# Sliding-window attention of a three-layer kernel: keys and values first, queries in quarters, output units and scalings at other steps

## The reference

```python
def swa_mixer(h, w_qkv, sinks, w_o):            # h: 256 x 1024, rms-normed
    qkv = h @ w_qkv                             # 1024 x (1024 + 128 + 128)
    q, k, v = split(qkv)                        # 16 heads of 64, 2 of 64, 2 of 64
    s = einsum(q, k_with_previous_block) * 64 ** -0.5
    logits = where(mask, s - slope * dist, -1e30)
    m = maximum(max(logits), sink)
    p = exp(logits - m)
    probs = p / (sum(p) + exp(sink - m))
    return einsum(probs, v_with_previous_block) @ w_o
h = h + swa_mixer(rms_norm(h), ...)
h = h + relu(rms_norm(h) @ w_up) ** 2 @ w_down
```

## Time and profile before

| | us |
|---|---|
| median of 3 runs | 976.29 (975.81 to 977.70) |
| the profiled execution | 973.68 |
| its span, first to last instruction | 971.9 |
| TensorE busy in the span | 944.2 |
| GpSimd busy | 675.4 |
| ScalarE busy | 499.6 |
| VectorE busy | 451.1 |

### The profile page before, as it was taken

The page is one execution under the profiler, slowest core; times in us unless marked ns, Lnnn a source line. Parts: engine busy times, 40 slices in busy tenths (PEclk is TensorE's granted clock), DMA queues, the critical chain, the costliest instruction groups (busy, mean ns, idle before and its releaser), DMA issues.

```text
span 971.9 us, 17687 instructions
## 1 busy us (share of the span) xinstructions
PE 944.2 (97%) x6878; PEld 880.7 (91%) x6878; DVE 451.1 (46%) x867; ACT 499.6 (51%) x702; POOL 675.4 (69%) x486
## 2 busy tenths in 40 slices
PE   5989999999999999999999999999998999999997
PEld 5989999999998889999999999888896789998886
DVE  3448753378443242666565566616627352221003
ACT  4675342673225465555666556555557346554331
POOL 4886645467555797966766676667697549889883
PEclk9999999999999999999999999999999999999999
DMA  8989858969734565744434444455663237666641
GB/s 242 164 214 103 185 104 85 161 109 100 145 107 128 184 195 158 211 131 134 149 114 146 138 146 132 131 171 186 173 204 102 70 107 225 207 176 209 198 133 43
DMA packets 131243, 146.30 MB, mean 151 GB/s; under 512 B 11022, under 2 KB 95960, under 8 KB 131160
## 3 DMA queue, kind: packets, MB, share of 16 engines
q1 hardware_dynamic: 129176, 140.64, 57.6%
q10 hardware_dynamic: 1984, 4.53, 1.4%
HBM read 144.10 MB, written 1.05 MB: 149 GB/s over the span
## 4 chain that ended last, share of the span: by engine, by line
PE 85%; DVE 4%; POOL 3%; ACT 3%; DMA 2%; issue 2%; SPq 1%; DVEq 0%; ACTq 0%; POOLq 0%
PE dense L546 23%; PE dense L547 22%; PE dense L548 22%; PE bank L908 3%; DMA raw<-in_w_in_even_dram 2%; PE bank L804 2%; PE bank L807 2%; POOL wlo L521 1%; POOL wlo L520 1%; PE bank L822 1%; POOL lg L506 1%; DVE cv L1739 1%; PE bank L897 1%; ACT whi L1153 1%; PE dense L615 1%
## 5 line engine op out<-in xcount | busy, mean ns | idle before, releaser
L521 POOL TENSOR_TENSOR wlo<-raw,whi 128x512 fp32r<-128x512 f32 (+1 forms) x263 | 411.7, 1571 | 29.0 <-ACT whi L1153 29.0
L520 POOL TENSOR_TENSOR wlo<-raw,whi 128x512 fp32r<-128x512 f32 x199 | 259.3, 1303 | 233.1 <-ACT whi L1153 220.9
L1153 ACT ACTIVATE whi<-raw 128x1024 fp32r<-128x1024 f32 x264 | 276.4, 1058 | 269.9 <-PE dense L548 233.7
L546 PE MATMUL dense<-x_hi,whi 128*128 128x256 f32 x1232 | 356.9, 290 | 11.1 <-POOL wlo L515 5.3
L547 PE MATMUL dense<-x_lo,whi 128*128 128x256 f32 x1232 | 344.5, 280 | 0.0
L548 PE MATMUL dense<-x_hi,wlo 128*128 128x256 f32 x1232 | 344.3, 279 | 0.0
L546 PEld LDWEIGHTS dense<-x_hi,whi 128*128 128x128 f32 x1232 | 232.4, 189 | 14.8 <-issue 7.4
L547 PEld LDWEIGHTS dense<-x_lo,whi 128*128 128x128 f32 x1232 | 232.4, 189 | 1.8 <-issue 1.7
L548 PEld LDWEIGHTS dense<-x_hi,wlo 128*128 128x128 f32 x1232 | 232.1, 188 | 0.0
L546 PE MATMUL dense<-whi,ya_hi 128*128 128x512 f32 x192 | 78.9, 411 | 0.7 <-issue 0.7
L548 PE MATMUL dense<-whi,ya_lo 128*128 128x512 f32 x192 | 75.9, 395 | 0.0
(11 more groups left out here) (323 smaller groups left out, 1425.5 us busy)
## 6 DMA issues: line engine op xcount, KB each, us to landing
raw<-in_w_in_odd_dram SPq DMA_DIRECT2D x64, 512.0 KB, 3.7
raw<-in_w_in_even_dram SPq DMA_DIRECT2D x32, 512.0 KB, 10.6
raw<-in_w_in_even_dram SPq DMA_DIRECT2D x64, 256.0 KB, 5.5
raw<-in_mlp_w_up_dram SPq DMA_DIRECT2D x32, 512.0 KB, 3.7
raw<-in_mlp_w_down_dram SPq DMA_DIRECT2D x32, 512.0 KB, 4.7
raw<-in_w_out_even_dram SPq DMA_DIRECT2D x16, 512.0 KB, 3.9
raw<-in_w_pl_gate_dram SPq DMA_DIRECT2D x16, 512.0 KB, 4.6
raw<-in_w_out_odd_dram SPq DMA_DIRECT2D x16, 512.0 KB, 4.0
```

Source lines behind the costliest of these rows:

```text
L520: pool.tensor_tensor(wlo[:, slot, 0:half], unit_slot(u)[:, 0:half], whi[:, slot, 0:half].bitcast(F32), ALU.subtract)
L521: pool.tensor_tensor(wlo[:, slot, first:2 * half], unit_slot(u)[:, first:2 * half], whi[:, slot, first:2 * half].bitcast(F32), ALU.subtrac ...
L546: pe.matmul(out_, lh, rh, start=start, stop=False, skip_group_check=True)
L1153: act.activation(whi[:, u % NSPL, :], unit_slot(u), ACT.Copy).then_inc(hi_done, 1)
```

## The change

Keys and values come first: units 0 to 3 are now keys and values. The queries follow in four quarters of 256 columns, two units each (4 to 11); the output units stay 12 to 19. Unit 4, 5 and 6 run ahead of the loop, units 7 to 11 at t = 0 to 4. Output units 12 to 15 run at t = 6, 7, 9 and 10 (before 6, 8, 9, 10). Quarter 0 has a bank of its own group, quarters 1 to 3 take turns in the two banks of another. VectorE takes quarter 0 out ahead of the loop and quarters 1, 2 and 3 at the end of steps 0, 2 and 4. The scores of step t wait for quarter t // 2. ScalarE rounds unit 11 + t at the start of steps 0 to 4, and units 16, 17, 18 and 19 at the end of steps 4, 5, 7 and 9. GpSimd does scaling i behind unit 12 + i for i = 0 to 5, and scalings 6 and 7 behind unit 18.

```diff
 load_list():
-    out += chunks("q_att", 0, 1) + chunks("kv_att", 0, 1) + chunks("q_att", 1, 1)
+    out += chunks("kv_att", 0, 1) + [("q_att", quarter, 0, 0) for quarter in range(4)]
 ...
-GROUPS += [("q_att", 0), ("kv_att", 0), ("q_att", 1)] + [("score", t) for t in range(8)]
+GROUPS += [("kv_att", 0), ("q_first", 0), ("q_rest", 0)] + [("score", t) for t in range(8)]
 ...
 weights():
+            if name == "q_att":
+                return wide(a["swa_w_qkv_2"][0][:, i * 2 * P:(i + 1) * 2 * P])
 ...
 GpSimd, behind the low part of unit u:
-                beside = u - FIRST_SPLIT[("q_att", 1, 0)] - AHEAD
-                for t in {1: (0,), 2: (1,), 3: (2, 3, 4), 4: (5, 6), 5: (7,)}.get(beside, ()):
+                beside = u - ATT_FIRST - 12
+                for t in (6, 7) if beside == 6 else (beside,) if 0 <= beside < 6 else ():
                     scales(t)
 ...
 TensorE, ahead of the loop (keys and values come first, then):
+            def q_unit(quarter, half):
+                if quarter == 0:
+                    bank = pair_of("q_first", 0)[0]
+                else:
+                    bank = pair_of("q_rest", 0)[(quarter - 1) % 2]
+                if half == 0 and quarter < 2:
+                    group_start("q_rest" if quarter else "q_first", 0)
+                if (quarter, half) == (3, 0):
+                    pe.wait_ge(att_in, 4)
+                wide_unit(half, bank, x_hi, x_lo).then_inc(split_used, 1)
 ...
-            dense_feature("q_att", 1, 0, x_hi, x_lo)
+            q_unit(0, 0)
+            q_unit(0, 1)
+            q_unit(1, 0)
             for t in range(11):
                 if t < 8:
-                    if t == 0:
-                        pe.wait_ge(att_in, 4)
-                    if t in (4, 6):
-                        pe.wait_ge(att_in, 5 + t // 6)
+                    if t % 2 == 0:
+                        pe.wait_ge(att_in, 3 + t // 2)
 ...
-                if t < 3:
-                    dense_feature("q_att", 1, t + 1, x_hi, x_lo)
-                if t in (6, 8, 9, 10):
-                    o_unit(t // 9, {6: 0, 8: 1, 9: 0, 10: 1}[t])
+                if t < 5:
+                    q_unit((t + 3) // 2, (t + 3) % 2)
+                if t in (6, 7, 9, 10):
+                    o_unit(t // 9, {6: 0, 7: 1, 9: 0, 10: 1}[t])
 ...
 ScalarE:
-                if t < 4:
-                    split_until(FIRST_SPLIT[("q_att", 1, 0)] + t + 1 + AHEAD)
+                if t < 5:
+                    split_until(ATT_FIRST + 7 + t + AHEAD)
 ...
-                if t in (4, 7, 9):
-                    split_until(FIRST_SPLIT[("o_att", 0, 0)] + {4: 6, 7: 7, 9: 8}[t])
+                if t in (4, 5, 7, 9):
+                    split_until(FIRST_SPLIT[("o_att", 0, 0)] + {4: 5, 5: 6, 7: 7, 9: 8}[t])
 ...
 VectorE, at the end of a step:
-                if t in (2, 3):
-                    queries(1, range(t - 2, t - 1))
+                if t in (0, 2, 4):
+                    queries(t // 2 + 1)
```

More of the change, by code:

```diff
@@ L95 @@
     UNITS_DONE[("vz", _i)] = UNITS_DONE[("hg_z", _i)]
+UNITS_DONE[("q_first", 0)] = UNITS_DONE[("q_att", 0)]
+UNITS_DONE[("q_rest", 0)] = UNITS_DONE[("q_att", 3)]
+ATT_FIRST = FIRST_SPLIT[("kv_att", 0, 0)]
 GROUPS = [("x_t", 0), ("x_t", 1)] + [(name, p) for p in range(GH // 2) for name in ("gd_kq", "gd_vz")] + [("hcbz", j) for j in range(KT)]
@@ L411, in weights @@
             tensor, layer, col = {"out_even": ("w_out_even", 0, i), "out_odd": ("w_out_odd", 0, i), "gate": ("w_pl_gate", i // 2, i % 2),
-                                  "q_att": ("swa_w_qkv_2", 0, i), "o_att": ("swa_w_o_2", 0, i),
+                                  "o_att": ("swa_w_o_2", 0, i),
                                   "up": ("mlp_w_up_2", 0, i), "down": ("mlp_w_down_2", 0, i)}[name]
@@ L973, in root_row @@
                 last.then_inc(row_spread, 1)
[L975 to L981, removed]
             group_start("kv_att", 0)
@@ L984, in _ @@
             for q in range(4):
+                pe.wait_ge(x2_ready, 4 + 2 * (q // 2) + 2)
                 wh, wl = unit_ready()
@@ L994, in _ @@
                 last.then_inc(split_used, 1)
+                if q == 0:
+                    x2_transposes(1, 1, 1)
+            pe.wait_ge(rstd_done, 1)
+            root_row()
+            def q_unit(quarter, half):
[8 more added lines that the diff above has]
+                wide_unit(half, bank, x_hi, x_lo).then_inc(split_used, 1)
             def o_unit(c, q):
@@ L1537, in _ @@
             layer_end(1)
-            split_until(FIRST_SPLIT[("q_att", 0, 0)] + 1 + AHEAD)
+            split_until(ATT_FIRST + 1 + AHEAD)
             rstd(0, RMS_EPS)
@@ L1543, in _ @@
             act.dma_start(gb[:, 0, :], a["final_norm_2"].rearrange("(o n) -> o n", o=1).broadcast_to([P, D])).then_inc(norm_rows, 16)
-            split_until(FIRST_SPLIT[("q_att", 1, 0)] + AHEAD)
+            split_until(ATT_FIRST + 6 + AHEAD)
             def sinks(t):
@@ L2148, in take_root_row, with queries @@
                 link(vec.tensor_copy(root[:, :], SB[0][:, 0:T]))
[L2150 to L2160, removed]
+            def queries(quarter):
+                group_ready("q_att", quarter)
+                name = "q_rest" if quarter else "q_first"
+                bank = pair_of(name, 0)[(quarter - 1) % 2 if quarter else 0]
+                for j in range(2):
+                    t = 2 * quarter + j
+                    link(vec.scalar_tensor_tensor(qa[:, t, :], bank[:, j * T:(j + 1) * T], AD ** -0.5 * 2.0 ** t, root[:, :], ALU.mult, ALU.mult),
+                         att_in if j else vec_chain)
+                if quarter in (0, 3):
+                    free(name, 0)
             row_stats(True)
             take_root_row(1)
-            queries(0)
             group_ready("kv_att", 0)
@@ L2173, in _ @@
             free("kv_att", 0)
+            queries(0)
             def scales(t):
```

## The result

| | median us | ratio to before | 95% interval |
|---|---|---|---|
| before | 976.43 (8 runs, one of them 1050.62) | | |
| the changed kernel | 980.19 (978.71 to 981.54, 8 runs) | 1.0036 | 1.0019 to 1.0052 |

What follows compares the result with a forecast made beforehand. TensorE, busy 944.2 of 971.9 us, was taken to bound the kernel, so only idle time counted: 7.6 us of waits after less 5.05 before, +2.5, plus 1.7 for the clock, +4.2; forecast 980.5 us, range 977.3 to 982.3.

Steps and rivals of the forecast that it cites:

- The front at no cost: Ahead of the loop: key/value loads coming first cost nothing, covered by about 4 us; first scores 5.6 us earlier.
- Steps 3 to 5: Attention loop: TensorE's waits of 1.74, 1.23 and 0.90 us for POOL's scaling go, about 0.05 left at the last.
- Step 6: Attention loop: 0.45 us idle ahead of the scores, then 0.97 instead of 0.67 ahead of the first output unit.
- Step 7: Attention loop: 0.25 us idle ahead of the second output unit, moved here, waiting for its input.
- Step 8: Loop step without scores or unit: seventh transposes wait 5.87 us for scaling 6, behind unit 18's rounding and low halves.
- The clock: Behind the long wait TensorE resumes at half clock, priced 1.7 us from the kernel's start, bounds 0 and 3.4.
- (a): Rival: the long wait comes but the clock stays whole; +2.5 us, 978.8 us; chance 0.27.
- The sum: Whole kernel: waits of 7.6 us less 5.05 give +2.5, with 1.7 for the clock +4.2 us.
- (b): Rival: all five old waits go and no new one decides; -5.05 us, 971.2 us; chance 0.08.
- (c): Rival: the new wait is half as long, some 3 us; -0.3 us, 976 us; chance 0.11.
- (d): Rival: the key/value loads are late after all; +3.0 us on top, 983.5 us; chance 0.04.

Runs made afterwards that it cites:

- run 1: The changed kernel with scaling 6 put back behind the low halves of unit 17, scaling 7 left behind unit 18's: 973.20 us, ratio to before 0.9977.
- run 5: The changed kernel with 20 unread 128-column matmuls put into the wait ahead of the seventh transposes: 977.62 us, ratio to before 1.0024.
- run 8: The program of run 7 with 8 unread matmuls put into the idle time near 66 us: 970.01 us, ratio to before 0.9939.
- run 2: The changed kernel with its second output unit moved back to step 8, scalings left as changed: 980.08 us, ratio to before 1.0043.
- run 3: The changed kernel with 32 unread 128-column matmuls put ahead of the seventh transposes: 980.45 us, ratio to before 1.0052.
- run 7: The changed kernel with scalings 5 to 7 behind unit 17's low halves and VectorE's low part of output 1 before the turned-probabilities copy: 971.80 us, ratio 0.9952.
- run 4: The kernel before with only scaling 6 moved from behind unit 17 to behind unit 18: 983.76 us, ratio to before 1.0080.

## Why the prediction was right, point by point

- **The front at no cost.** Right: TensorE has no wait between the first key/value unit and the scores of step 5. The first scores come 5.2 us earlier against the root row, not 5.6, in the main because three query matmuls took 0.36 us there instead of 0.35. The 718.4 in the text was wrong as a clock reading (722.12), by this 0.4 and by the 3.3 us ahead of the root row.
- **Steps 3 to 5 lose their waits.** Right, all three, with 0.06 left at step 5 against 0.05.
- **Step 6.** 0.77 and 0.81 against 0.45 and 0.97. VectorE's timeline of the changed kernel (queries of quarter 3, scores of pair 5, the reciprocal that marks their end):

```profile
746.12 0.88 DVE L2172 SCALAR_TENSOR_TENSOR qa<-dense,root 128x256 f32<-128x256 f32 x2
...
747.29 0.48 DVE L2214 CUSTOM_DVE_ANT_0 lg<-con,dense,lg 128x256 f32<-128x256 f32 x1 [0.28 <-DVE qa L2172]
...
749.30 0.18 DVE L2196 RECIPROCAL rsum<-st_att 128x4 f32<-128x4 f32 x1 [0.21 <-DVE st_att L2214]
```

The scores did start right behind the queries, but 0.28 us after their end, and the banks were free 2.0 us later (749.29) and not 1.8. The place was right and the handovers were left out.
- **Step 7.** 0.20 against 0.25.
- **Step 8.** 5.75 against 5.87, by the chain that was named, and undone by the one line that was named (run 1). All waits together: 0.06 + 0.77 + 0.81 + 0.20 + 5.75 = 7.6, as forecast; less 5.05 is +2.5.
- **The clock.** Forecast 1.7 from the start's row, found 1.6 from the transposes and products behind the wait, and 1.56 by run 5. It was the weakest step, since that row could not tell a fall from a clock that had never risen, and no row of before showed a fall. That the size came out so near is in part luck. One premise was wrong: the longest idle time inside the kernel before is not 1.74 us but the 2.55 near 66 us, shown under run 8. It left the clock whole too, so it would have raised the chance of rival (a), and the traces of the other runs show that it does not always. What I said to look for was off: the slow stretch was over before the 512-column matmuls, and the granted clock did show it (0.50).
- **The sum.** +4.2 forecast, +4.5 between the landmarks, +3.5 (1.9 to 5.1) in the ratio. From the first scores to the end of the loop the sum said 55.9 + 1.7 = 57.6, the trace says 57.55. Two slips changed nothing: the bounds of the forecast add up to 982.7 at the top (976.3 + 3.0 + 3.4) and not to the 982.3 of the range, and the chances to 0.76 slower and 0.08 faster, not 0.75 and 0.09.

Of the rivals, (a) fell by the windows and by run 5, (b) is what remains when scaling 6 is put back, though 2.2 us instead of 5.05, since the waits of steps 6 and 7 stay and one of 0.77 comes in step 9, (c) and (d) have nothing left to explain.

## What to carry to other kernels

An engine that takes its work in order and does two jobs (here weight halves and scalings) needs each piece of one job placed against the moment that its neighbour of the other job becomes possible, and not only against the moment that it is wanted. Scaling 6 could have started two and a half microseconds before it was wanted (by run 1 at about 759.1 in the changed kernel's time, against 761.66) and been done 0.9 us ahead of it, and stood behind a unit that was not rounded yet. When a dense unit is moved ahead to fill one wait, look at which step has now no work of its own, and follow the release of that step back by hand. When the two spans of a comparison differ by more than the medians, measure between landmarks inside the traces before explaining anything.

## What the runs showed that I had not expected

- The length of an idle time does not settle whether the clock falls. The same wait of 2.30 to 2.33 us was followed by half clock in runs 1, 2, 3 and 7 and by the whole clock in runs 4 and 5. A wait of 1.74 us left it whole in the execution of before and was followed by a fall in run 4. Behind 3.64, 4.61, 5.20 and 5.75 us it was half each time. So short waits inside dense work cost more than their length in some executions; what decides it stays open.
- A fall costs about 1.6 us in both places where it can be priced (1.56 in the attention by run 5, 1.5 to 1.6 near 66 us), and it can be bought off with matmuls that compute nothing, if they end before the wait does.
- A 128-column float32 matmul of this kind counts as two instructions and 0.226 us in the trace (7.24 us for 32), where a transpose of the same size takes 0.13 (six in 0.8) and a product of the same size into half the array 0.09 (twelve in 1.07).
